# Opening of a two-block transformer kernel: modulation rows loaded ahead of the input

## The chip, the cores and the metric

The kernel runs on one core of a Trainium2 chip. The metric is the device time of one execution in microseconds (us). Three executions of the kernel before took 3241.57, 3241.45 and 3239.81, median 3241.45.

TensorE (PE) multiplies matrices, VectorE (DVE), ScalarE (ACT) and GpSimd (POOL) work elementwise, and SyncE (SP) issues the transfers (DMA). Each engine runs its own instructions in order and waits on semaphores for the others.

## The reference

The model has two blocks over 512 rows of 1024 features. The first holds two layers: an even one (convolution and an RWKV mixer) and an odd one (attention); the second holds a mixer, a product-key expert layer with 16384 experts and a gated embedding. What this case touches is the beginning of the first layer:

```python
cond = jax.nn.silu(c)
mod = cond @ ada_w[l] + ada_b[l]
shift, scale, gate = jnp.split(mod, 3, axis=-1)
h = rms_norm(x, norm_g[l]) * (1.0 + scale[:, None, :]) + shift[:, None, :]
z = h @ even_w_in[j]
```

`cond` is a vector of 1024, `ada_w[0]` is 1024 x 3072, `x` is 512 x 1024, `even_w_in` is 1024 x 7296.

## The kernel before, in words

Features lie on the 128 partitions: `xT` holds the input as eight tiles of 128 x 512. Weights come as units of 128 x 1024 float32, 512 KB each, in the order in which `schedule()` numbers them. That function writes one list of pieces; each engine walks the list and does its own part of each piece, so the list is the order on every engine.

**Modulation rows.** A group `g` of 512 outputs of `cond @ ada_w` takes four units, `ada(0, g)`. TensorE multiplies a unit by two columns of `cond` (line 762, one output row of 512 on a partition, two matmuls a unit, four in the profile). After the fourth unit ACT copies the row (line 1199), TensorE turns it into four columns (line 772, the piece `turned`) and VectorE adds the bias (line 1635). Groups 0 and 1 are the shift, 2 and 3 the scale. So the shift and the scale need 16 units, numbers 0 to 15. `turned_late` puts each `turned` one unit behind its row. The gate's groups 4 and 5 come later.

**Statistics of the input.** For each tile of `xT`, ACT squares (line 1210) and VectorE adds into `msum` (line 1649). `stat` is TensorE's column sum with `ones` (line 782), the mean and root on VectorE and ACT and a diagonal from `ident`; `bcast` spreads it over the partitions (line 791). `norm` is the normalization: for each of eight tiles VectorE scales (line 1697), ACT makes the high part (line 1244), VectorE the low part (line 1709).

**Weights of the dense products.** They are split in a high and a low part: ACT copies the unit as float32r into one of three slots `wsp` (`hi`, line 1178), POOL subtracts (`lo`, line 2439), and TensorE uses three matmuls of 128 x 512 for each of eight blocks (lines 732 to 734). Unit 16 is the mixing product `mu`, units 17, 18 and 19 are `r`, `k` and `v` of head pair 0. ACT's copy of unit n+1 (`hi_to`) stands at the beginning of a piece of unit n, ahead of the copy of a row.

**Places.** The first `NE` = 11 units go to places of their own, in buffers that the RWKV stage uses later (`early`); those behind them go round a ring of `RING` = 3. SP loads units in order (`load_to`, line 2578); a unit from `NE + RING` on waits until the unit three before it has been used. `vec` is the table of all small vectors, `c` among them. `vec`, `ones` and `ident` raise one semaphore, `consts_in`, and their readers wait for all three. Behind `norm` stands `rw_begin`, where VectorE, POOL and SP wait for all engines (`fence`, `all_done`).

Of the kernel before, what the change touches and what calls it, by code (L numbers as in the profile page):

```python
# [20 lines left out]
KT = 8  # L21
CH = 4
# [123 lines left out]
def schedule():  # L146
# [9 lines left out]
    def ada(l, g):  # L156
        return [("ada", l, g, kp, 24 * l + 4 * g + kp) for kp in range(4)]
# [53 lines left out]
    order += [("square", "n0", k) for k in range(KT)]  # L211
    order.append(("stat", "n0"))
    number(ada(0, 0))
    order.append(("bcast", "n0"))
    number(turned_late([x for g in range(1, 4) for x in ada(0, g)], ("turned", 0, 0)))
# [114 lines left out]
    z = [0]  # L330
# [79 lines left out]
def build(nc, t):  # L410
    ORDER, UNITS, FIRST, OF = schedule()
    NU = len(UNITS)
    with ExitStack() as ctx:
# [39 lines left out]
        def chunked(ap):  # L453
            return ap.rearrange("p (c n) -> p c n", c=CH)
# [4 lines left out]
        def kept_set():  # L459
            return {"dd": a(CH), "tt": [chunked(a(512)) for _ in range(3)]}  # L460
# [33 lines left out]
        early = [*(abk[0][:, i * 1024:(i + 1) * 1024] for i in range(4)), *xts, *krs, lup]  # L494
# [94 lines left out]
        consts_in, x_in, rw_in, yc_in, yb_in, ag_in = (sem(f"s_{n}") for n in ("c", "x", "rw", "yc", "yb", "ag"))  # L589
# [134 lines left out]
        def tensor_program(pe):  # L724
# [50 lines left out]
            def stat(tag):  # L775

                out, free = (inv_b if tag == "n0" else all_b).open(("stat", tag), V, "mean", tag)
                w.wait_ge(*free)
                w.wait_ge(consts_in, 48)
                w.wait_ge(vector_done, V("acc", tag, 7))  # L780
                for b in range(4):
                    r = pe.matmul(out[:, b:b + 1], acc_of[tag][:, b * 128:(b + 1) * 128], ones[:, 0:1], start=True, stop=True)
                r.then_inc(tensor_done, T.step("sum", tag))
# [386 lines left out]
        def scalar_program(act):  # L1170
# [15 lines left out]
            def start():  # L1186
                w.wait_ge(consts_in, 48)
                act.activation(cond[:, :], cols("c"), ACT.Silu).then_inc(scalar_done, A.step("cond"))
# [58 lines left out]
            def norm(tag):  # L1247
                shift = {"n0": mod[:, 0, 0:8], "n1": mod[:, 1, 0:8]}.get(tag)
                for k in range(KT):
                    high(tag, k, shift)  # L1250
# [349 lines left out]
        def vector_program(dve):  # L1600
# [22 lines left out]
            def start():  # L1623
                for b in dense.banks:
                    dve.memset(b["ap"], 0.0).then_inc(vector_done, V.step("clear"))
                w.wait_ge(consts_in, 48)
# [941 lines left out]
        def sync_program(sp):  # L2568
# [12 lines left out]
            def start():  # L2581
                sp.dma_start(vec[:, :], t["vec"][:, :]).then_inc(consts_in, 16)
                sp.dma_start(ones[:, :], t["ones"][:, :]).then_inc(consts_in, 16)
                sp.dma_start(ident[:, :], t["ident"][:, :]).then_inc(consts_in, 16)
                sp.dma_start(xT[:, :, :], t["xT"].rearrange("(k p) s -> p k s", p=128)).then_inc(x_in, 16)
# [258 lines left out]
```

## Time and profile before

| | |
|---|---|
| median of 3 runs | 3241.45 us (3239.81 to 3241.57) |
| profiled execution | 3239.83 us, of which its span 3237.9 us |
| TensorE busy | 3065.3 us, 95% |
| VectorE, ScalarE, GpSimd busy | 67%, 38%, 28% |
| mean granted TensorE clock | 0.979 of full speed |
| transferred | 378.81 MB, mean 117 GB/s |

The span begins with the first instruction and ends with the last; times in the profile count from its start. The chain that ended last consists of TensorE for 73% and VectorE for 19%. TensorE's busy share is at least 90% in every fortieth of the span from the fourth on, but for one of 80% and the last of 70%; the first three have 60, 70 and 80%. The granted clock is the share of full speed that the throttle gave TensorE. A timeline row gives start and duration of a merged group of instructions, and in brackets how long the engine sat idle before it and what ended that.

### The profile page before, as it was taken

What the parts mean: (1) busy time and instruction counts of PE and PEld (TensorE: products, weight loads), DVE (VectorE), ACT (ScalarE), POOL (GpSimd) and SP (SyncE); (2) the same over time, 40 slices, a digit from 0 to 9 for tenths busy, and PEclk for the clock granted to TensorE, in tenths of its full rate; (3) what the DMA queues carried; (4) which work ended last, traced back from release to release, by engine and by line L of the source; (5) the groups of instructions that cost most, each with busy time, mean ns of one, the idle gap of its engine ahead of it and who ended that gap; (6) DMA issues with size and microseconds to landing.
All of it is one profiled execution on the core that took longest, in us unless ns stands there. A gap on an engine that the chain in (4) does not pass through costs nothing.

```text
span 3237.9 us, 39785 instructions
## 1 busy us (share of the span) xinstructions
PE 3065.3 (95%) x16086; PEld 2407.6 (74%) x16086; DVE 2184.1 (67%) x3497; ACT 1243.6 (38%) x1815; POOL 892.5 (28%) x550
## 2 busy tenths in 40 slices
PE   6789999999999899999999999999999999999997
PEld 3467776667767566787887788878888888888885
DVE  3688899867789866565889899556665444444454
ACT  3334444435333455323333466532233222233333
POOL 2343343332334110043445433232222111111100
PEclk9999999999999899999999999999999999999999
DMA  5211111235312111232234376775564333333331
GB/s 208 91 69 47 46 46 53 73 105 179 101 65 85 40 39 33 85 117 91 79 130 137 118 235 202 240 247 191 179 201 150 111 119 122 124 123 123 118 117 39
DMA packets 165334, 378.81 MB, mean 117 GB/s; under 512 B 10656, under 2 KB 77216, under 8 KB 165024
## 3 DMA queue, kind: packets, MB, share of 16 engines
q1 hardware_dynamic: 165152, 376.28, 34.6%
q8 instruction: 127, 2.08, 0.3%
q14 instruction: 55, 0.45, 0.0%
HBM read 318.04 MB, written 58.20 MB: 116 GB/s over the span
## 4 chain that ended last, share of the span: by engine, by line
PE 73%; DVE 19%; ACT 4%; POOL 2%; DMA 2%; issue 1%; SPq 0%; DVEq 0%; ACTq 0%; POOLq 0%
PE ps L732 20%; PE ps L734 20%; PE ps L733 20%; DVE rw L1777 3%; DVE oh L2359 2%; PE ps L1121 2%; PE ps L1049 2%; DVE at L2097 2%; DVE ai L2095 1%; PE ps L1029 1%; PE ps L908 1%; DVE at L2085 1%; POOL wsp L2439 1%; POOL pk L2551 1%; PE ps L1039 1%
## 5 line engine op out<-in xcount | busy, mean ns | idle before, releaser
L732 PE MATMUL ps<-hT,wsp 128*128 128x512 f32 x2016 | 825.9, 410 | 35.2 <-POOL wsp L2439 20.1
L2439 POOL TENSOR_TENSOR wsp<-ring,wsp 128x1024 fp32r<-128x1024 f32 x207 | 518.3, 2506 | 1083.9 <-ACT wsp L1178 1060.9
L734 PE MATMUL ps<-hT,wsp 128*128 128x512 f32 x2016 | 793.2, 393 | 0.0
L733 PE MATMUL ps<-hT,wsp 128*128 128x512 f32 x2016 | 792.9, 393 | 0.0
L732 PEld LDWEIGHTS ps<-hT,wsp 128*128 128x128 f32 x2016 | 382.8, 190 | 145.5 <-issue 28.7
L734 PEld LDWEIGHTS ps<-hT,wsp 128*128 128x128 f32 x2016 | 382.6, 190 | 83.6
L733 PEld LDWEIGHTS ps<-hT,wsp 128*128 128x128 f32 x2016 | 383.9, 190 | 77.9 <-issue 6.0
L2558 POOL TENSOR_TENSOR ex<-ex 128x512 fp32r<-128x512 f32 x128 | 176.1, 1390 | 831.4 <-ACT ex L1559 831.4
L1178 ACT ACTIVATE wsp<-ring 128x1024 fp32r<-128x1024 f32 x311 | 322.2, 1051 | 100.8 <-PE ps L734 78.8
L2383 DVE TENSOR_TENSOR xT<-ps,xT 128x512 f32<-128x512 f32 x256 | 174.8, 688 | 261.4 <-PE ps L734 261.4
L732 PE MATMUL ps<-ex 128*128 128x512 f32 x808 | 314.8, 390 | 2.0 <-DVE ex L1611 2.0
L734 PE MATMUL ps<-ex 128*128 128x512 f32 x808 | 315.1, 390 | 0.0
L733 PE MATMUL ps<-ex 128*128 128x512 f32 x808 | 314.6, 389 | 0.0
L1777 DVE SCALAR_TENSOR_TENSOR rw<-rw,vec 128x512 f32<-128x512 f32 x240 | 243.0, 1013 | 5.3
L1178 ACT ACTIVATE ex<-ring 128x1024 fp32r<-128x1024 f32 x121 | 126.2, 1054 | 305.6 <-PE ps L734 197.9
L2373 DVE TENSOR_TENSOR ex<-ex 128x512 f32<-128x512 f32 x128 | 102.8, 824 | 188.1 <-ACT ex L1556 131.1
L1611 DVE TENSOR_TENSOR ex<-ring,ex 128x1024 fp32r<-128x1024 f32 x121 | 164.0, 1355 | 95.6 <-ACT ex L1178 95.6
L732 PEld LDWEIGHTS ps<-ex 128*128 128x128 f32 x808 | 151.8, 188 | 34.8 <-DVE ex L1611 2.8
L733 PEld LDWEIGHTS ps<-ex 128*128 128x128 f32 x808 | 151.8, 188 | 31.9
L734 PEld LDWEIGHTS ps<-ex 128*128 128x128 f32 x808 | 151.8, 188 | 31.6
L1559 ACT ACTIVATE ex<-ex 128x512 fp32r<-128x512 f32 x128 | 80.0, 632 | 240.2 <-DVE ex L2373 240.2
L1611 DVE TENSOR_TENSOR wsp<-ring,wsp 128x1024 fp32r<-128x1024 f32 x104 | 132.0, 1269 | 25.8 <-ACT wsp L1178 25.6
(395 smaller groups left out, 4754.2 us busy)
## 6 DMA issues: line engine op xcount, KB each, us to landing
ring<-in_eu SPq DMA_DIRECT2D x128, 512.0 KB, 3.3
ring<-in_ev SPq DMA_DIRECT2D x128, 512.0 KB, 3.5
gd<-oh SPq DMA_DIRECT2D x8, 4096.0 KB, 15.0
ex<-gd SPq DMA_DIRECT2D x32, 1024.0 KB, 6.6
ring<-in_ein SPq DMA_DIRECT2D x57, 512.0 KB, 3.3
ring<-in_oin SPq DMA_DIRECT2D x39, 512.0 KB, 3.2
ring<-in_ada SPq DMA_DIRECT2D x37, 512.0 KB, 3.2
ex<-zd SPq DMA_DIRECT2D x17, 1024.0 KB, 9.0
```

The source lines that it names most:

```text
L732: pe.matmul(out, W[0], R[0], start=first, stop=False)
L733: pe.matmul(out, W[0], R[1], start=False, stop=False)
L734: return pe.matmul(out, W[1], R[0], start=False, stop=last)
L1049: r = pe.matmul(out, Vs[:, s, :], PTs[h % 2][:, s, :], start=s == 0, stop=s == 3)
L1178: act.activation(split_of(n)[:, 0, :], raw_of(n), ACT.Copy).then_inc(scalar_done, A.step("hi", n))
L1559: act.activation(agb[c % 2][:, 0, j, :], exb[2 + (c * JC + j) % 3], ACT.Copy).then_inc(scalar_done, A.step("agh", c, j))
L1611: dve.tensor_tensor(s[:, 1, :], raw_of(n), s[:, 0, :].bitcast(F32), ALU.subtract).then_inc(vector_done, V.step("lo", n))
L1777: dve.scalar_tensor_tensor(out=y, in0=u[:, k:k + S], scalar=col("conv_w", m * TAPS + k), in1=y, op0=ALU.mult, op1=ALU.add).then_inc(vector ...
L2373: dve.tensor_tensor(exb[2 + i % 3].rearrange("p (b t) -> p b t", t=TG), x.rearrange("p (b t) -> p b t", t=TG), g[:, j, :, :], ALU.mult).th ...
L2383: dve.tensor_tensor(xT[:, dt, :], all_b.at["v", c, dt], xT[:, dt, :], ALU.add).then_inc(vector_done, V.step("v", c, dt))
L2439: pool.tensor_tensor(s[:, 1, :], raw_of(i), s[:, 0, :].bitcast(F32), ALU.subtract).then_inc(pool_done, G.step("lo", i))
L2558: pool.tensor_tensor(agb[c % 2][:, 1, j, :], exb[2 + (c * JC + j) % 3], agb[c % 2][:, 0, j, :].bitcast(F32), ALU.subtract).then_inc(pool_d ...
```

## The change

It has six parts. (1) `vec` gets a semaphore of its own, `vec_in`; the first instructions of ACT (`cond`) and VectorE (`omka`) wait for that, and `stat` waits for the other two constants. (2) SP issues `vec`, units 0 to 4, `xT`, units 5 to 7, `ones`, `ident`, and then the rest. (3) The list has units 0 to 4 and the first `turned` ahead of the squares, units 5 to 12 behind them, then `stat`, units 13 and 14, `bcast`, and unit 15. (4) Three more early places, in the three kept sets of the RWKV stage, whose three 512-column tiles are now one piece of 1536 with the four-column tile behind it; `NE` is 14, so unit 14 is the first in the ring. (5) ACT's next weight copy, of unit 17, stands between the fourth and the fifth tile of `norm`. (6) Line numbers move by two.

```diff
--- before.py
+++ after.py
@@ -208,11 +208,8 @@
     def gates(tiles):
         return [x for m in tiles for x in dense("agate", m, 16 + m)]
 
-    order += [("square", "n0", k) for k in range(KT)]
-    order.append(("stat", "n0"))
-    number(ada(0, 0))
-    order.append(("bcast", "n0"))
-    number(turned_late([x for g in range(1, 4) for x in ada(0, g)], ("turned", 0, 0)))
+    rows = turned_late([x for g in range(4) for x in ada(0, g)])
+    number([*rows[:6], *(("square", "n0", k) for k in range(KT)), *rows[6:15], ("stat", "n0"), *rows[15:18], ("bcast", "n0"), *rows[18:]])
     order.append(("norm", "n0"))
     order.append(("rw_begin",))
     number(dense("mu", 0, 48))
@@ -457,7 +454,8 @@
         a = Stage("rw")
 
         def kept_set():
-            return {"dd": a(CH), "tt": [chunked(a(512)) for _ in range(3)]}
+            turned = a(1536)
+            return {"all": turned, "tt": [chunked(turned[:, i * 512:(i + 1) * 512]) for i in range(3)], "dd": a(CH)}
 
 
         yT, varT, gsT, sgT = (a(512) for _ in range(4))
@@ -491,7 +489,7 @@
                       for i in range(2)) for z in abk]
         XTs = [z.rearrange("p (e c n) -> p e c n", e=2, c=CH) for z in xts[0:2]]
         X = xts[2].rearrange("p (e c n) -> p e c n", e=2, c=CH)
-        early = [*(abk[0][:, i * 1024:(i + 1) * 1024] for i in range(4)), *xts, *krs, lup]
+        early = [*(abk[0][:, i * 1024:(i + 1) * 1024] for i in range(4)), *xts, *krs, lup, *(z["all"][:, 0:1024] for z in sets)]
         NE = len(early)
         Xo = msum.rearrange("p (c e n) -> p c e n", c=CH, e=2)
         Sbd, Su, x1n, SA = (small[:, 2 * i:2 * i + 2, :].rearrange("p a n -> p (a n)") for i in range(4))
@@ -586,7 +584,7 @@
 
         tensor_done, vector_done, scalar_done, pool_done = (sem(f"s_{n}") for n in ("pe", "dve", "act", "pool"))
         T, V, A, G = Marks(tensor_done), Marks(vector_done), Marks(scalar_done), Marks(pool_done)
-        consts_in, x_in, rw_in, yc_in, yb_in, ag_in = (sem(f"s_{n}") for n in ("c", "x", "rw", "yc", "yb", "ag"))
+        vec_in, consts_in, x_in, rw_in, yc_in, yb_in, ag_in = (sem(f"s_{n}") for n in ("vec", "c", "x", "rw", "yc", "yb", "ag"))
         unit_in = [sem(f"s_w{i}") for i in range(RING)]
         early_in = [sem(f"s_e{i}") for i in range(NE)]
         yt_out = [sem(f"s_yt{i}") for i in range(2)]
@@ -776,7 +774,7 @@
 
                 out, free = (inv_b if tag == "n0" else all_b).open(("stat", tag), V, "mean", tag)
                 w.wait_ge(*free)
-                w.wait_ge(consts_in, 48)
+                w.wait_ge(consts_in, 32)
                 w.wait_ge(vector_done, V("acc", tag, 7))
                 for b in range(4):
                     r = pe.matmul(out[:, b:b + 1], acc_of[tag][:, b * 128:(b + 1) * 128], ones[:, 0:1], start=True, stop=True)
@@ -1184,7 +1182,7 @@
                     at["hi"] += 1
 
             def start():
-                w.wait_ge(consts_in, 48)
+                w.wait_ge(vec_in, 16)
                 act.activation(cond[:, :], cols("c"), ACT.Silu).then_inc(scalar_done, A.step("cond"))
 
             def ada(l, g, kp, n):
@@ -1247,6 +1245,8 @@
             def norm(tag):
                 shift = {"n0": mod[:, 0, 0:8], "n1": mod[:, 1, 0:8]}.get(tag)
                 for k in range(KT):
+                    if tag == "n0" and k == 4:
+                        hi_to(at["hi"])
                     high(tag, k, shift)
 
 
@@ -1623,7 +1623,7 @@
             def start():
                 for b in dense.banks:
                     dve.memset(b["ap"], 0.0).then_inc(vector_done, V.step("clear"))
-                w.wait_ge(consts_in, 48)
+                w.wait_ge(vec_in, 16)
                 dve.tensor_scalar(omka[:, :], cols("k_a"), -1.0, 1.0, ALU.mult, ALU.add).then_inc(vector_done, V.step())
 
             def ada(l, g, kp, n):
@@ -2579,10 +2579,12 @@
                     at["load"] += 1
 
             def start():
-                sp.dma_start(vec[:, :], t["vec"][:, :]).then_inc(consts_in, 16)
+                sp.dma_start(vec[:, :], t["vec"][:, :]).then_inc(vec_in, 16)
+                load_to(5)
+                sp.dma_start(xT[:, :, :], t["xT"].rearrange("(k p) s -> p k s", p=128)).then_inc(x_in, 16)
+                load_to(8)
                 sp.dma_start(ones[:, :], t["ones"][:, :]).then_inc(consts_in, 16)
                 sp.dma_start(ident[:, :], t["ident"][:, :]).then_inc(consts_in, 16)
-                sp.dma_start(xT[:, :, :], t["xT"].rearrange("(k p) s -> p k s", p=128)).then_inc(x_in, 16)
                 load_to(NE + RING - 1)
                 sp.dma_start(bones[:, :], t["bones"][:, :]).then_inc(rw_in, 16)
                 sp.dma_start(cen, t["cen"][:, :]).then_inc(rw_in, 16)
```

SP, the queue of transfers, from its beginning; `rw_..` are the early places, and `in_ada` are the row units. Before:

```order
L2582 DMA vec<-in_vec 128x487
L2583 DMA ones<-in_ones 128x128
L2584 DMA ident<-in_ident 128x128
L2585 DMA xT<-in_xT 128x8x512
L2578 DMA rw_43<-in_ada 128x1024 x4
L2578 DMA rw_21<-in_ada 128x1024
L2578 DMA rw_49<-in_ada 128x1024
L2578 DMA rw_22<-in_ada 128x1024
L2578 DMA rw_33<-in_ada 128x1024
L2578 DMA rw_5<-in_ada 128x1024
L2578 DMA rw_34<-in_ada 128x1024
L2578 DMA rw_20<-in_ada 128x1024
```

After:

```order
L2582 DMA vec<-in_vec 128x487
L2578 DMA rw_39<-in_ada 128x1024 x4
L2578 DMA rw_21<-in_ada 128x1024
L2578 DMA rw_43<-in_ada 128x1024
L2584 DMA xT<-in_xT 128x8x512
L2578 DMA rw_22<-in_ada 128x1024
L2578 DMA rw_33<-in_ada 128x1024
L2578 DMA rw_5<-in_ada 128x1024
L2586 DMA ones<-in_ones 128x128
L2587 DMA ident<-in_ident 128x128
L2578 DMA rw_34<-in_ada 128x1024
L2578 DMA rw_20<-in_ada 128x1024
```

Units 0 to 4 have moved ahead of `xT`, and `ones` and `ident` from ahead of `xT` to behind unit 7.

SP again, around the first units of the ring: `in_ein` are the units of the dense products, the first of them 16. Before:

```order
L2578 DMA rw_20<-in_ada 128x1024
L2578 DMA ring<-in_ada 128x1024 x3
L2587 DMA bones<-in_bones 128x128
L2588 DMA rw_29<-in_cen 128x128
L2578 DMA ring<-in_ada 128x1024 [waits s_pe] x2
L2578 DMA ring<-in_ein 128x1024 [waits s_pe] x3
L2578 DMA ring<-in_ein 128x1024 [waits s_pool]
```

After:

```order
L2578 DMA rw_35<-in_ada 128x1024
L2578 DMA rw_40<-in_ada 128x1024
L2578 DMA rw_37<-in_ada 128x1024
L2578 DMA ring<-in_ada 128x1024 x2
L2578 DMA ring<-in_ein 128x1024
L2589 DMA bones<-in_bones 128x128
L2590 DMA rw_29<-in_cen 128x128
```

Before, two row units and the first `in_ein` wait for TensorE; after, only units behind 16 wait.

TensorE, on both sides of the column sums (`msum` and `ones`, 128x1) and of the broadcast (128x512); `s_e0` to `s_e13` are the landings of units 0 to 13. Before, from the beginning of its queue:

```order
L782 MATMUL ps0<-ones,msum 128x1 [waits s_dve,s_c]
L782 MATMUL ps0<-ones,msum 128x1 x3
L762 MATMUL ps6<-rw_43,cond 1x512 [waits s_e0,s_act]
L762 MATMUL ps6<-rw_43,cond 1x512
L762 MATMUL ps6<-rw_43,cond 1x512 [waits s_e1]
L762 MATMUL ps6<-rw_43,cond 1x512
L762 MATMUL ps6<-rw_43,cond 1x512 [waits s_e2]
L762 MATMUL ps6<-rw_43,cond 1x512
L762 MATMUL ps6<-rw_43,cond 1x512 [waits s_e3]
L762 MATMUL ps6<-rw_43,cond 1x512
L791 MATMUL ps1<-msum,ones 128x512 [waits s_dve]
L762 MATMUL ps7<-rw_21,cond 1x512 [waits s_e4]
```

The same engine from unit 11 on. After:

```order
L760 MATMUL ps6<-rw_35,cond 1x512
L760 MATMUL ps7<-rw_40,cond 1x512 [waits s_e12]
L760 MATMUL ps7<-rw_40,cond 1x512
L780 MATMUL ps0<-ones,msum 128x1 [waits s_dve,s_c]
L780 MATMUL ps0<-ones,msum 128x1 x3
L770 MATMUL ps4<-vec,rw_4 128x1 [waits s_act]
L770 MATMUL ps4<-vec,rw_4 128x1 x3
L760 MATMUL ps7<-rw_37,cond 1x512 [waits s_e13]
L760 MATMUL ps7<-rw_37,cond 1x512
L760 MATMUL ps7<-ring,cond 1x512 [waits s_w0]
L760 MATMUL ps7<-ring,cond 1x512
L789 MATMUL ps1<-msum,ones 128x512 [waits s_dve]
```

The column sums have moved from the first place of the queue to behind unit 12 (`s_e12`), and the broadcast from behind unit 3 (`s_e3`) to behind unit 14 (`s_w0`).

ACT, from unit 16's copy (`wsp<-ring`, `s_w2`) through the eight tiles of `norm`. Before:

```order
L1199 ACTIVATE rw_4<-ps6 128x512 [waits s_pe]
L1178 ACTIVATE wsp<-ring 128x1024 [waits s_w2]
L1199 ACTIVATE rw_4<-ps7 128x512 [waits s_pe]
L1244 ACTIVATE hT<-rw_9,mod 128x512 [waits s_pe,s_dve]
L1244 ACTIVATE hT<-rw_10,mod 128x512 [waits s_dve]
L1244 ACTIVATE hT<-rw_24,mod 128x512 [waits s_dve]
L1244 ACTIVATE hT<-rw_4,mod 128x512 [waits s_dve]
L1244 ACTIVATE hT<-rw_9,mod 128x512 [waits s_dve]
L1244 ACTIVATE hT<-rw_10,mod 128x512 [waits s_dve]
L1244 ACTIVATE hT<-rw_24,mod 128x512 [waits s_dve]
L1244 ACTIVATE hT<-rw_4,mod 128x512 [waits s_dve]
L1178 ACTIVATE wsp<-ring 128x1024 [waits s_pool,s_w0,s_act,s_dve]
```

After:

```order
L1215 ACTIVATE cr<-cr 128x4 [waits s_dve]
L1176 ACTIVATE wsp<-ring 128x1024 [waits s_w2]
L1197 ACTIVATE rw_4<-ps7 128x512 [waits s_pe]
L1242 ACTIVATE hT<-rw_9,mod 128x512 [waits s_pe,s_dve]
L1242 ACTIVATE hT<-rw_10,mod 128x512 [waits s_dve]
L1242 ACTIVATE hT<-rw_24,mod 128x512 [waits s_dve]
L1242 ACTIVATE hT<-rw_4,mod 128x512 [waits s_dve]
L1176 ACTIVATE wsp<-ring 128x1024 [waits s_w0]
L1242 ACTIVATE hT<-rw_9,mod 128x512 [waits s_dve]
L1242 ACTIVATE hT<-rw_10,mod 128x512 [waits s_dve]
L1242 ACTIVATE hT<-rw_24,mod 128x512 [waits s_dve]
L1242 ACTIVATE hT<-rw_4,mod 128x512 [waits s_dve]
```

The copy of unit 17 (`s_w0`) stands behind four tiles now, and the copy of unit 18 (`s_w1`) is the first behind the fence.

## Rows read from the trace of the kernel before

**Rows 1.** The page: busy time, share of the span and instructions of TensorE.

```profile
PE 3065.3 (95%) x16086; PEld 2407.6 (74%) x16086; DVE 2184.1 (67%) x3497; ACT 1243.6 (38%) x1815; POOL 892.5 (28%) x550
```

**Rows 2.** Chain of waits, 0 to 120 us: start us, duration us, what.

```profile
2.13 10.48 DMA xT<-in_xT
...
19.49 1.84 PE ps L782 x8
...
21.33 3.44 PE ps L762 x16
...
24.77 1.05 PE ps L791 x2
...
27.76 1.84 PE ps L762 x16
...
39.21 1.06 ACT wsp L1178
...
40.90 1.19 PE ps L772 x8
...
42.75 2.06 DVE rw L1697 x3
...
53.44 1.07 ACT wsp L1178
...
54.67 2.35 POOL wsp L2439
...
57.06 0.50 PE ps L732
...
73.45 0.24 PE ps L734
```

**Rows 3.** Timeline of SP's issues: start us, us, line, transfer, count.

```profile
2.60 0.67 SPq L2578 DMA_DIRECT2D rw<-in_ada  x1
...
13.39 0.44 SPq L2578 DMA_DIRECT2D ring<-in_ada  x1
...
13.87 2.90 SPq L2578 DMA_DIRECT2D ring<-in_ada  x1
...
33.18 0.80 SPq L2578 DMA_DIRECT2D ring<-in_ada  x2
```

**Rows 4.** Transfers issued at 2.60, 13.39, 13.87: size, us to landing.

```profile
rw<-in_ada SPq DMA_DIRECT2D x1, 512.0 KB, 11.3
...
ring<-in_ada SPq DMA_DIRECT2D x1, 512.0 KB, 15.6
...
ring<-in_ada SPq DMA_DIRECT2D x1, 512.0 KB, 16.5
```

**Rows 5.** Timeline of ACT's table load and TensorE's last row units (idle before, releaser).

```profile
16.92 1.28 ACT L1215 ACT_TABLE_LOAD   x1
...
30.27 1.05 PE L772 MATMUL ps<-vec,rw 128*128 128x1 f32 x8 [0.68 <-ACT rw L1199]
...
36.38 1.03 PE L762 MATMUL ps<-ring,cond 128*1 128x512 f32 x4 [0.47 <-DMA ring<-in_ada]
...
37.66 1.03 PE L762 MATMUL ps<-ring,cond 128*1 128x512 f32 x4 [0.25 <-DMA ring<-in_ada]
```

**Rows 6.** Stretches: us, busy (instructions) PE, PEld, DVE, ACT, POOL; PEclk, DMA share, GB/s.

```profile
0.00:5.00 5.00, 0.00 (x0) 0.00 (x0) 0.97 (x2) 1.28 (x1) 0.20 (x4) 1.00 0.51 123
5.00:10.00 5.00, 0.00 (x0) 0.00 (x0) 0.17 (x1) 0.21 (x1) 0.00 (x0) 1.00 1.04 351
20.00:25.00 5.00, 5.00 (x24) 1.93 (x24) 1.03 (x3) 0.33 (x2) 0.00 (x0) 1.00 1.03 419
30.00:35.00 5.00, 3.95 (x34) 2.34 (x36) 0.17 (x2) 0.82 (x2) 0.00 (x0) 1.00 0.15 53
45.00:50.00 5.00, 4.14 (x11) 2.76 (x12) 5.00 (x8) 2.73 (x4) 0.00 (x0) 0.66 0.06 23
```

**Rows 7.** Timeline of ACT in the normalization, one copy of eight.

```profile
46.17 0.72 ACT L1244 ACTIVATE hT<-rw,mod 128x512 fp32r<-128x512 f32 x1 [0.60 <-DVE rw L1697]
```

## The prediction, on record before the changed kernel ran

> **What bounds the kernel now.** I read the page first: TensorE is busy 95% of the span [rows 1], so almost everything after the opening is a line of work behind TensorE, and a few microseconds saved in front of it come out at the end. Then the chain of waits over the first 60 us, where every edit lies [rows 2]. Call the sixteen 512 KB units of the first modulation U0 to U15 and the two weight units behind them U16 (mixing, "mu") and U17 (first r tile). The reader should see four legs. The input lands at 12.6. Squares, their sum and TensorE's column sums end at 21.3, and only then does TensorE begin U0 to U3 (21.33). From there it works through the rows until it reaches units that have not come: U14, U15 and U16 go into the ring of three, and SP issues U14 only at 33.18, when U11 has been used [rows 3]. TensorE starts U14 at 36.38 and U15 at 37.66, both on the DMA [rows 5]. Last, U16 lands at 39.2, ACT copies it (1.06), and only behind that copies the last row; TensorE turns it at 40.90 and the normalization starts at 42.75. It ends at 53.4; then ACT copies U17, POOL subtracts (2.35), and TensorE starts r at 57.06.
>
> So the transfers stand still from about 30 to 33 (0.15 of the DMA engines busy in 30 to 35 [rows 6]), with three units still to come, and TensorE stands idle until 19.5 with units long landed.
>
> **How fast units come.** U0 was issued at 2.60 and landed 11.3 later, 13.9. U12 was issued at 13.39 and took 15.6, landing at 29.0; U13 at 13.87, taking 16.5, at 30.4 [rows 3, 4]. That is (30.4 - 13.9)/13 = 1.27 us a unit, which is 524 KB at the 419 GB/s of the window 20 to 25 [rows 6]. They come in the order of issue: U0 1.3 behind the input.
>
> **The change part by part.**
>
> *Order of the transfers.* What must land before U12 is the same set of bytes before and after: vec, ones, ident, xT, U0 to U12. Only the start differs. In the first 5 us the queue moved 123 GB/s, since three small transfers came first, against 351 in the next 5 [rows 6]. With U0 as the second transfer up to about 3 us of that could run at the higher rate: (351 - 123) x 3 = 0.68 MB at most, from which I allow 0.5 MB, 1.2 us at 419 GB/s. The bounds of this credit are 0 and 1.2; ones and ident still have to pass later, so I take 0.5. U12 lands at 28.5 (27.8 to 29.0). Each further unit adds 1.27 without a wait, because with 14 early places the ring starts at U14 and holds U14, U15, U16: U13 29.8, U14 31.1, U15 32.3, U16 33.6, instead of 36.4, 37.7 and 39.2.
>
> *Input behind U4.* It lands five units later less the credit: 12.6 + 5 x 1.27 - 0.5 = 18.5. The column sums, which wait for the sum of squares, began at 19.5, 6.9 behind the landing [rows 2]; now they could from 25.4. The column sums are placed behind U12 (29.4), so 4 us of slack hide this. The two small copies that ACT now makes behind the squares (0.61 each) wait for U7 and U11, not for the squares, and the ACT table load for the root (1.28 [rows 5]) lies behind U11's copy: U11 at 27.2, its matmuls and the copy until 28.8, the load until 30.1, before the column sums end at 31.2. Nothing is added.
>
> *TensorE's line.* From U12 it is in order and full. U12 0.86 (3.44/4, the slow pace at 21.33), column sums 1.84, turning row 2 1.05, U13 and U14 at the fast pace of 0.46 each (1.84/4), broadcast 1.05, U15 alone 1.03 [rows 2, 5]: 28.5 + 0.86 + 1.84 + 1.05 + 0.92 + 1.05 + 1.03 = 35.25. U16's copy on ACT ends at 33.6 + 1.06 = 34.7, so it no longer holds the last row back. ACT copies the row (0.65, of which TensorE's pause of 0.68 before the turning at 30.27 is the mark [rows 5]), 35.9; the turning starts, and the normalization follows 1.85 behind its start (42.75 - 40.90): 37.8. Gain of this leg: 42.75 - 37.8 = 4.95, say 5.0. What is late next is this serial line and no longer a transfer.
>
> *U17's copy among the normalization.* ACT's copies there take 0.72, with 0.60 of idle time between them [rows 7]; a copy of 1.07 [rows 2] between the fourth and the fifth delays the fifth by 1.07 - 0.60 = 0.47, and VectorE reads the fifth only two steps (2.6 us) on. Behind it on ACT's queue stand four more such copies, each with 0.60 to catch up. U17 waits for U14's use (about 33); U14 itself took 3.2 from its issue to TensorE's start [rows 3, 5], so U17 is there by 37, ahead of about 42. Free. At the end POOL starts at 0.1 after the normalization instead of 54.67 - 53.44 = 1.23 after: a gain of 1.1, carried on since TensorE then works without a hole from 57.06 until 73.7 in the chain. If ACT's copy were late, this term would be 0.
>
> *The rest.* The vector semaphore lets ACT and VectorE start on vec alone, before U0 is there: nothing. Waiting for 32 instead of 48 on ones and ident: they now follow U7 and land near 23, needed at 29.4. The kept set with its 4 columns last moves three tiles by 16 bytes; one set loses what another gains in alignment, and no row tells tiles at such offsets apart; I take 0, with -0.3 to +0.3. The ring's slot numbers stay (11 and 14 have the same remainder by 3), so all later loads wait as before.
>
> Sum: 5.0 + 1.1 = 6.1. Against the profiled execution's 3239.83 (span 3237.9) that is 3233.7; the median of the runs shown, 3241.45, lies 1.6 above it, so 3235.4.
>
> Bounds of the unknown terms. Early end: U12 at 27.8, all of TensorE fast; then U16's copy rules (32.9 + 1.06 = 34.0), normalization at 36.5: 6.2 + 1.1 = 7.3. Late end: no credit (29.0) and every piece slow: 0.86 + 1.84 + 1.19 + 1.72 + 2.1 + 1.03 + 0.61 + 1.99 = 11.3, so 40.3: 2.4 + 1.1 = 3.5. (2.1 is the broadcast doubled, an estimate from its 1.05.)
>
> **Two rules beside the rows.** The profile grants TensorE its full 2.4 GHz in 20 to 25, yet four units take 3.44 there and 1.84 from 27.76 on [rows 2, 6]; in 45 to 50, behind a pause, the granted clock is 0.66. The Trainium skill (TensorE: Matmul & The Clock Gate, Part 1) says that the array is at 1.2 GHz by default and activity releases it, and that the recorded clock events can't be fully trusted. By that rule work that comes in short bursts, as the rows now do, could stay slow to the end of the line, which is rival B; the slow pace at 21.33 agrees.
>
> The Trainium skill (DMA: Bandwidth & Descriptors, Where 436 GB/s comes from) puts a core's limit from HBM at about 358 GB/s. The trace disagrees with 419. By the rule a unit would cost 1.46 instead of 1.27, and U16 would come 0.8 later against U12, still ahead of the last row's copy or level with it.
>
> **The rivals.**
> A. TensorE is fast when U12 comes. For it: at the slow pace it has holes of only 0.4 in the 1.27 us of a unit, and from 27.76 to 38.7 it paused as much and stayed fast [rows 2, 5]. Then the column sums take about 1.0, the line ends at U16's copy (34.7), the copy of the row at 35.3, normalization at 37.2: 5.55 + 1.1 = 6.65, and up to 7.3 with the credit. 3234.8.
> B. TensorE stays slow over the whole line. For it: idle from about 10 to 19 between U4 and U5, and short bursts after. Against: from U12 on it is busy without a hole, and at 21.3 the same sort of work became fast within 5 us. With the slow pieces of the late end, 28.5 + 11.3 = 39.8: 2.95 + 1.1 = 4.0. 3237.4.
> C. The opening gives nothing: the transfers end when they did, slowed by the matmuls that now read units while others land, and only U17's copy pays: 1.1, 3240.3. Against it: in 20 to 25 TensorE was busy throughout and the queue moved 419 GB/s [rows 6].
> D. Slower: the input starves behind and among eleven queued units. If it shared the queue with the nine units issued behind it instead of coming in order, its landing L would drive everything: L + 6.9 (sum of squares), + 1.84 + 1.05 + 0.92 + 1.05 + 1.03 + 0.65 + 1.85 = L + 15.3. That equals 42.75 + 1.1 at L = 28.6; with all units landing first, L is about 33.6, normalization at 48.9, 6.1 - 1.1 = 5.0 slower: 3246.5. Against it: the input landed 1.3 before U0 with eleven units behind it [rows 2, 4].
>
> **How the numbers follow.** The forecast has 0.50, A 0.22, B 0.18, C 0.06, D 0.04. The forecast's own range, with the 1.8 us between the three runs shown, is 3234.0 to 3236.8. For 8 in 10 it reaches through A and B with their spread: 3232.4 to 3238.6. A measurement of this kernel can tell about 0.2%, 6.5 us, from no change; that bound lies at 3235.0, just inside the forecast. Faster: 0.33 of the forecast, three quarters of A and a little of B: 0.40. Slower: 0.03. Same: 0.57.
>
> **What would show it.** U14's matmuls start without a DMA wait other than the pace, by about 33; U16 lands near 33.6; column sums start behind U12 near 29.4; the normalization starts near 37.8, ends 10.7 later; POOL's first subtraction of r starts within 0.2 of its end; r near 51. It would be wrong if the normalization starts outside 36.5 to 40.3, if the pace of landing differs from 1.27, if TensorE's clock falls for long behind 51, or if the time from r's first matmul to the end differs by over 2 us.

## The result, and the profile after

Eight executions of the changed kernel took 3223.62 to 3240.20 us, median 3228.4. Eight of the kernel before took 3232.87 to 3242.44, median 3238.36 (the three shown ahead of the prediction are among them). The ratio is 0.9975, interval 0.9964 to 0.9986, which is 8.1 us less (4.5 to 11.7); the two medians by themselves differ by 10.0. The profiled execution took 3233.98 against 3239.83, with spans of 3232.1 and 3237.9.

The forecast was 3235.4 (3232.4 to 3238.6) and a gain of 6.1. The time lies below the range, and the gain is one that a measurement tells from no change, to which the prediction gave 0.40.

In code line 762 is now 760, 772 is 770, 782 is 780, 791 is 789, 1199 is 1197 and 1178 is 1176; lines 732 to 734 are 730 to 732. The page's span, its line of busy times, and the granted clock in 40 slices. The mean granted clock of this execution was 0.975, where it was 0.979 before, and TensorE's busy time is 13.2 us longer:

```profile
span 3232.1 us, 39783 instructions
...
PE 3078.5 (95%) x16086; PEld 2413.8 (75%) x16086; DVE 2176.2 (67%) x3497; ACT 1243.6 (38%) x1815; POOL 891.8 (28%) x550
...
PEclk9889999999999999999999999999999999999999
```

The chain of waits of the changed kernel (start us, duration us, what), which answers to [rows 2]:

```profile
18.84 13.57 DMA ring<-in_ein
...
32.44 1.06 ACT wsp L1176
...
33.49 0.49 ACT rw L1197
...
34.03 1.07 PE ps L770 x8
...
35.32 0.63 DVE gsc L1639
...
35.97 2.06 DVE rw L1697 x3
...
46.76 2.38 POOL wsp L2439
...
49.18 0.50 PE ps L730
```

The input and TensorE's column sums are gone from the chain. It now consists of SP's issues one after the other from 0.74 to 18.84, the transfer of U16 (issued 18.84, landed 32.4), ACT's copy of U16, its copy of the row behind it, the turning, VectorE, and the normalization, which starts at 35.97 instead of 42.75: 6.8 us earlier. From the normalization's start to r's first matmul it takes 13.2 instead of 14.3, so r starts at 49.18 instead of 57.06: 7.9 us, which the measured 8.1 agrees with.

TensorE's timeline (start, duration, line, matmuls and count, in brackets the idle time and what ended it), to compare with [rows 5] and the slow start at 21.33 in [rows 2]:

```profile
4.78 1.87 PE L760 MATMUL ps<-rw,cond 128*1 128x512 f32 x4 [4.78 <-DMA rw<-in_ada]
...
12.88 1.03 PE L760 MATMUL ps<-rw,cond 128*1 128x512 f32 x4
...
19.39 3.62 PE L760 MATMUL ps<-rw,cond 128*1 128x512 f32 x12 [5.48 <-DMA rw<-in_ada]
...
27.33 1.03 PE L760 MATMUL ps<-rw,cond 128*1 128x512 f32 x4 [0.25 <-DMA rw<-in_ada]
...
28.29 1.05 PE L780 MATMUL ps<-ones,msum 128*128 128x1 f32 x8
...
31.13 1.13 PE L789 MATMUL ps<-msum,ones 128*128 128x512 f32 x2
...
32.19 1.03 PE L760 MATMUL ps<-ring,cond 128*1 128x512 f32 x4
```

U0 lands at 4.7, 3.5 us behind its issue. Six row units are issued ahead of the input, not five: `load_to(5)` loads U0 to U5, and TensorE works on the sixth at 12.88, before the input lands. In the same way `load_to(8)` puts `ones` and `ident` behind U8, not U7. The description of the change and the prediction have both wrong by one unit. U12 is there at 27.33 (forecast 28.5), the column sums take 1.05 and not 1.84, and U15 ends at 33.2 (forecast 35.3).

The stretches that answer to the first and the third of [rows 6] (busy of PE, PEld, DVE, ACT, POOL; granted clock, DMA share, GB/s):

```profile
0.00:5.00 5.00, 0.22 (x2) 0.12 (x4) 1.14 (x3) 1.49 (x2) 0.20 (x4) 1.00 0.65 200
20.00:25.00 5.00, 4.90 (x26) 1.34 (x24) 4.25 (x8) 2.96 (x6) 0.00 (x0) 0.80 1.03 408
```

In the first 5 us the queue moves 200 GB/s instead of 123. TensorE has paused from 13.9 to 19.4 and its granted clock is 0.80 in 20 to 25, but when U12 comes it works at the fast pace.

### The profile page after: what moved, and what is told of

It reads as the page before. It is cut to its first block, busy times and chain, and to the rows that moved or that the text cites. A ratio compares the mean times of both kernels' runs of the same rounds, so it can differ in the third digit from the quotient of the medians.

```text
span 3232.1 us, 39783 instructions
## 1 busy us (share of the span) xinstructions
PE 3078.5 (95%) x16086; PEld 2413.8 (75%) x16086; DVE 2176.2 (67%) x3497; ACT 1243.6 (38%) x1815; POOL 891.8 (28%) x550
## 4 chain that ended last, share of the span: by engine, by line
PE 71%; DVE 19%; ACT 4%; POOL 2%; DMA 2%; issue 1%; SPq 1%; DVEq 0%; ACTq 0%
PE ps L730 20%; PE ps L732 19%; PE ps L731 19%; DVE rw L1777 3%; DVE oh L2359 2%; PE ps L1119 2%; PE ps L1047 2%; DVE at L2097 2%; DVE ai L2095 1%; PE ps L1027 1%; PE ps L906 1%; DVE at L2085 1%; POOL wsp L2439 1%; POOL pk L2551 1%; PE ps L1037 1%
```

## The experiments

All of them are compared by two numbers: the start of r's first matmul in one profile, which an opening moves, and the timed difference to the kernel before on the same chip, with its interval. Single executions of a kernel here differ by up to 19 us (28 to 32 executions of the kernel before beside each group of experiments: 3230.2 to 3249.7), so the timed differences have intervals of 3.2 to 4.9 us to either side. The profiles scatter too. In the five that begin with the same nine units and the input, and in which TensorE waits for U12, U12's matmuls start from 27.2 to 28.1 (with the later start of one of them taken off), and the two profiles of the changed kernel have r at 49.18 and 49.67. One profile tells differences of 1 us and more, not of tenths.

### The changed kernel again

No edit.

> The changed kernel once more. Both theories: r's first matmul at 49.2 us, as in its first profile (57.06 before). They part in the stretch from there to ACT's table load of line 1275, which took 52.3 us before and 55.8 in the first profile of the changed kernel, with TensorE's granted clock at half from 82.9 to 97.4. Theory 1 (the opening's 7.9 us reach the end, and where the clock falls behind it differs from one execution to the next): this profile may show either length, and the timed difference to the kernel before is near -8. Theory 2 (the new opening itself makes the clock fall there and gives 3.5 us back): the stretch is 55 to 56 again and the timed difference is near -4.5.

Measured: ratio 0.9957 (0.9942 to 0.9972), 13.9 us less (9.1 to 18.8). r starts at 49.67. Here TensorE was slow ahead of U12 (granted clock 0.50 in 20 to 25 and 0.66 in 25 to 30), its line ended behind ACT's copy of U16, and the normalization followed TensorE:

```profile
32.62 1.06 ACT L1176 ACTIVATE wsp<-ring 128x1024 fp32r<-128x1024 f32 x1 [1.42 <-DMA ring<-in_ein]
33.26 1.03 PE L760 MATMUL ps<-ring,cond 128*1 128x512 f32 x4
...
36.47 2.06 DVE L1697 SCALAR_TENSOR_TENSOR rw<-xT,gsc,ps 128x512 f32<-128x512 f32 x3
```

That is 3.85 from the start of the copy to the normalization, where the first profile has 3.53.

The stretch from r's start to ACT's table load of line 1275 took 55.0 (55.8 in the first profile of the changed kernel). That looked like theory 2, but the timed difference is far from the 4.5 us that it asks for, and the other kernels settle it. The stretch came out as 52.3 in the kernel before, 51.9, 51.9, 51.9, 53.2 and 53.4 in five others, and 55.1, 55.1, 55.1, 55.1 and 56.6 in five, among these one with the opening time of before (the old list, below: 55.1). So it comes out short or long whatever the opening. In the changed kernel and then in the kernel before, the stretches at the same place of the program:

```profile
80.00:85.00 5.00, 2.12 (x12) 0.18 (x6) 0.00 (x0) 0.00 (x0) 0.00 (x0) 0.85 0.72 253
85.00:90.00 5.00, 4.03 (x9) 1.33 (x6) 1.23 (x2) 4.02 (x5) 2.34 (x1) 0.50 0.49 175
90.00:95.00 5.00, 5.00 (x17) 4.33 (x16) 3.56 (x6) 0.38 (x1) 2.37 (x1) 0.50 0.51 161
95.00:100.00 5.00, 5.00 (x19) 4.00 (x19) 4.79 (x10) 0.00 (x0) 1.83 (x2) 0.79 0.10 40
```

```profile
92.00:97.00 5.00, 3.44 (x6) 0.59 (x6) 0.69 (x1) 3.29 (x4) 2.31 (x1) 0.66 0.65 237
```

After TensorE's pause at this place (it waits for a modulation unit) the granted clock is half, for some 14 us in the changed kernel and 3.4 in the kernel before. These times are estimates from the mean granted clock of the stretch, with the two levels 0.5 and 1. The same working for all thirteen profiles orders them: 3.3 or 3.4 us at half clock in the four whose stretch took 51.9 to 52.3, 6.8 in the six with 53.2 to 55.1, and 10.3 to 13.7 in the three with 55.1, 55.8 and 56.6.

### The whole opening 7 us later

```diff
 def start():                       # VectorE
+    for _ in range(2):
+        dve.memset(abk[0], 0.0).then_inc(vector_done, V.step("late"))
+        own()
 def start():                       # SP
+    w.wait_ge(vector_done, V("late"))
     sp.dma_start(vec[:, :], ...)
```

> The changed kernel with its whole opening pushed back: VectorE first fills a 128x4096 tile twice (3.5 us each), and SP issues nothing before that. No other instruction moves. Theory 1 (a shift of the opening reaches the end whole): r's first matmul near 56.2, 7 us later, and a time 7 us above the changed kernel, about that of the kernel before (difference to it -1). Theory 2 (the shift is partly given back or lost behind the opening): a time 3 to 4 above the changed kernel.

Measured: r starts at 58.32, 9.1 later than in the changed kernel and 1.3 later than before; VectorE's two fills come ahead of everything and took more than I had allowed. Timed 0.9991 (0.998 to 1.0001), 2.9 us below the kernel before (-6.5 to +0.3). The changed kernel gained 13.9 beside it, so a delay of the opening does reach the end; the intervals are too wide to say that all of it does.

### The old list with the new transfers

```diff
-rows = turned_late([x for g in range(4) for x in ada(0, g)])
-number([*rows[:6], *(("square", "n0", k) ...), *rows[6:15], ("stat", "n0"), *rows[15:18], ("bcast", "n0"), *rows[18:]])
+order += [("square", "n0", k) for k in range(KT)]
+order.append(("stat", "n0"))
+number(ada(0, 0))
+order.append(("bcast", "n0"))
+number(turned_late([x for g in range(1, 4) for x in ada(0, g)], ("turned", 0, 0)))
 def stat(tag):                     # ACT
+    w.wait_ge(consts_in, 32)
```

> The changed kernel's transfers, places and semaphores with the old list: squares and column sums ahead of the first row unit on TensorE. With the input landing at 18.1 the column sums begin at 25.0, and the 15 row units behind them go at the pace of before, slow for the first four. Theory 1 (the new place of the row units in the list carries the gain, the transfers alone would lose): normalization from 44.4 instead of 36.0, r from 57.6, a time 8.4 above the changed kernel and 0.5 above the kernel before. Rival (transfers alone carry it, since U16's landing at 32.4 is what bounds): normalization within 1 of 36.0.

Measured: 1.0003 (0.9991 to 1.0015), no gain. r at 57.22. From its chain and TensorE's timeline:

```profile
24.76 1.84 PE ps L783 x8
...
44.01 2.06 DVE rw L1701 x3
...
26.53 3.23 PE L763 MATMUL ps<-rw,cond 128*1 128x512 f32 x16
```

The column sums begin at 24.76 and take 1.84, the first four units take 3.2, and the normalization starts at 44.01 (44.4 expected). The new transfers and places with the old list lose 1.3 us at that point; with the old list, the old transfers and the places alone (below) it starts at 38.30. The list is what makes the new order of transfers pay.

### The two constants first again

```diff
 sp.dma_start(vec[:, :], ...).then_inc(vec_in, 16)
+sp.dma_start(ones[:, :], ...).then_inc(consts_in, 16)
+sp.dma_start(ident[:, :], ...).then_inc(consts_in, 16)
 load_to(5)
 sp.dma_start(xT[:, :, :], ...)
 load_to(8)
-sp.dma_start(ones[:, :], ...).then_inc(consts_in, 16)
-sp.dma_start(ident[:, :], ...).then_inc(consts_in, 16)
```

> The changed kernel with the two constants of 64 KB (ones, ident) issued right behind vec again instead of behind U8. Theory 1 (the small transfers at the beginning cost the first 5 us their rate, and their going away is the missing 1.2 us of credit): U12 lands at 28.5 instead of 27.3, and r starts 1.2 later, 50.4. Rival (they cost what their 128 KB are worth, 0.3 us, or the two issues of 0.47, and the credit has another source): U12 at 27.3 to 27.9 and r at 49.2 to 49.9.

Measured: 0.9976 (0.9965 to 0.9986), r at 51.70, 2.5 later than in the changed kernel. Its stretches 3 to 4 and 20 to 25:

```profile
3.00:4.00 1.00, 0.00 (x0) 0.00 (x0) 0.17 (x1) 0.21 (x1) 0.00 (x0) 1.00 0.36 78
20.00:25.00 5.00, 3.72 (x12) 0.28 (x12) 3.35 (x5) 4.82 (x9) 0.00 (x0) 0.52 1.03 419
```

The same stretch 3 to 4 in the changed kernel:

```profile
3.00:4.00 1.00, 0.00 (x0) 0.00 (x0) 0.17 (x1) 0.21 (x1) 0.00 (x0) 1.00 1.00 385
```

Its U12, U15 and `gsc`:

```profile
28.78 1.03 PE L760 MATMUL ps<-rw,cond 128*1 128x512 f32 x4 [0.25 <-DMA rw<-in_ada]
...
35.28 1.03 PE L760 MATMUL ps<-ring,cond 128*1 128x512 f32 x4
...
38.29 0.17 DVE L1639 SCALAR_TENSOR_TENSOR gsc<-mod,vec 128x8 f32<-128x8 f32 x1
```

U12 comes at 28.78, 1.45 later than in the changed kernel and 0.7 to 1.6 later than in the five profiles above: theory 1, with its size open. Between 3 and 4 the queue moves 78 GB/s, where the changed kernel moves 385. The other profiles bear that out: 108, 115 and 131 in the three others with the constants in front, 356 to 420 in the seven with row units there. Over the first 25 us the mean is 341 GB/s against 350, though, which is 0.2 MB or 0.55 us at the pace; where the rest of the 1.45 comes from is open. The other microsecond of r has another cause: TensorE's granted clock is 0.66 in 30 to 35, where U13, U14 and the broadcast run, so U15 starts at 35.28 and the normalization 1.1 later than U16's landing asks for (ACT's copy at 33.85 + 3.53 = 37.4; it starts at 38.49).

### Without the copy of unit 17 in the normalization

```diff
 for k in range(KT):
-    if tag == "n0" and k == 4:
-        hi_to(at["hi"])
     high(tag, k, shift)
```

> The changed kernel without the copy of unit 17 between the fourth and the fifth tile of the normalization. Theory (the copy is free there and saves ACT's copy behind the end): normalization starts at 36.0 and ends near 46.7 as in the changed kernel, POOL's subtraction starts 1.23 behind its end instead of 0.1, r's first matmul at 50.3 instead of 49.2. Rival (the copy costs VectorE something inside): the normalization is shorter than 10.7 and r is at 49.9 or less.

Measured: 0.9989 (0.9976 to 1.0002). The normalization starts at 36.92 and r at 51.24, which is 14.3 behind it, as before the change; with the copy it is 13.2. So the term of 1.1 holds. The late start of the normalization goes with the clock again (0.66 granted in 30 to 35), from TensorE's timeline:

```profile
31.02 1.91 PE L789 MATMUL ps<-msum,ones 128*128 128x512 f32 x2
...
32.86 1.87 PE L760 MATMUL ps<-ring,cond 128*1 128x512 f32 x4
```

The broadcast and U15 take 1.91 and 1.87, where the changed kernel takes 1.13 and 1.03.

### Eleven early places

```diff
-early = [..., *krs, lup, *(z["all"][:, 0:1024] for z in sets)]
+early = [..., *krs, lup]
```

> The changed kernel with 11 early places instead of 14, so that U14, U15 and U16 wait for the use of U11, U12 and U13. Theory (places matter since the ring's waits stop the transfers): U11 is used at 27.1, U14 is there 3.2 later at 30.4, U15 at 31.7; U13 is used only at 30.6, behind the column sums, so U16 comes at 33.9 instead of 32.4; normalization 3.54 behind that, 37.4, r 50.7. Rival (TensorE's line hides it): normalization within 0.5 of 36.0.

Measured: 0.9997 (0.9985 to 1.0009), r at 52.42, 3.2 later. From its chain:

```profile
31.72 3.95 DMA ring<-in_ein
...
35.69 1.06 ACT wsp L1176
...
39.22 2.06 DVE rw L1697 x3
```

U16 is issued when U13 has been used, at 31.72, and lands at 35.7. I had expected 33.9: U13 used at 30.6 and 3.2 for the transfer. It was used 1.1 later, and the transfer took 3.95. The mechanism is the theory's, its size 1.8 larger.

### The input first

```diff
-load_to(5)
 sp.dma_start(xT[:, :, :], ...)
```

> The changed kernel with the input issued right behind vec, ahead of all row units; list, places and semaphores as in the changed kernel. Theory 1 (the sum of bytes until U16 counts, not which come first; the list does the rest): input at 11.5, U0 at 12.8, U12 at 27.3, U16 at 32.4, normalization at 36.0 to 36.5. Theory 2 (rows ahead of the input are needed, since TensorE is idle for longer and slow when U12 comes, or ACT's first row copy holds the squares up): normalization at 37.5 or later.

Measured: 0.9967 (0.9954 to 0.9979), r at 49.98. TensorE's U0 and U12, and the chain:

```profile
12.63 4.88 PE L760 MATMUL ps<-rw,cond 128*1 128x512 f32 x16 [12.63 <-DMA rw<-in_ada]
...
28.17 1.03 PE L760 MATMUL ps<-rw,cond 128*1 128x512 f32 x4 [0.25 <-DMA rw<-in_ada]
...
33.23 1.06 ACT wsp L1176
...
36.77 2.07 DVE rw L1697 x3
```

U0 comes at 12.63 instead of 4.78, and all that it costs is 0.8 us, the 0.8 by which U12 and U16 come later. That is hardly more than equal openings differ by (U16's copy at 33.13 in the kernel with unit 16 on VectorE, below, and at 33.23 here), so a cost isn't shown. The order of the list counts, with enough units behind the input; which transfer is first counts for less than 1 us.

### Column sums, broadcast and the last row's copy earlier

```diff
-number([*rows[:6], ..., *rows[6:15], ("stat", "n0"), *rows[15:18], ("bcast", "n0"), *rows[18:]])
+number([*rows[:6], ..., *rows[6:13], ("stat", "n0"), *rows[13:15], ("bcast", "n0"), *rows[15:]])
 def ada(l, g, kp, n):              # ACT, for the unit (0, 3, 3)
-    hi_to(n + 1)
     ... act.activation(rowT, ...)
+    hi_to(n + 1)
```

> The changed kernel with the column sums behind U10 and the broadcast behind U12, and ACT's copy of the last row ahead of its copy of U16. Theory (what bounds the changed kernel is U16's landing at 32.4, its copy and the row's copy behind it): U15 lands at 31.2 and is used by 32.3, its row is copied by 32.9, the turning takes 1.05, normalization at 35.0 instead of 36.0, r at 48.2; a time 1 below the changed kernel, which the timing can't tell. Rival (U16's copy, now later, holds the first mu product back): normalization early but r not.

Measured: 0.9976 (0.9963 to 0.9989), r at 49.22: nothing gained. The turning does start 1.4 earlier, but:

```profile
33.62 2.34 POOL L2443 TENSOR_TENSOR wsp<-ring,wsp 128x1024 fp32r<-128x1024 f32 x1 [33.17 <-ACT wsp L1176]
...
33.93 2.04 DVE L1643 SCALAR_TENSOR_TENSOR gsc<-mod,vec 128x8 f32<-128x8 f32 x1
...
36.01 2.06 DVE L1701 SCALAR_TENSOR_TENSOR rw<-xT,gsc,ps 128x512 f32<-128x512 f32 x3
```

The small `gsc` operation of VectorE (128x8) takes 2.04 us and ends with POOL's subtraction of U16. In the kernel before and in the changed kernel:

```profile
40.35 2.34 POOL L2439 TENSOR_TENSOR wsp<-ring,wsp 128x1024 fp32r<-128x1024 f32 x1 [39.91 <-ACT wsp L1178]
...
42.31 0.40 DVE L1639 SCALAR_TENSOR_TENSOR gsc<-mod,vec 128x8 f32<-128x8 f32 x1
```

```profile
33.57 2.34 POOL L2439 TENSOR_TENSOR wsp<-ring,wsp 128x1024 fp32r<-128x1024 f32 x1 [33.13 <-ACT wsp L1176]
...
35.32 0.62 DVE L1639 SCALAR_TENSOR_TENSOR gsc<-mod,vec 128x8 f32<-128x8 f32 x1
```

It takes 0.40 and 0.62 there, and each time the normalization starts within 0.06 us of POOL's end (42.69 and 42.75, 35.91 and 35.97). In the kernel with the constants first, POOL is done before, and it takes 0.17 (row above). The Trainium skill (SBUF — State Buffer, SBUF: two separate sides) says that an operation of VectorE with two inputs in SBUF and a GpSimd operation that reads SBUF exclude each other, and the later one waits to the end. The trace agrees: `gsc` reads `mod` and `vec`, both in SBUF, and the operation just before it, with one input in PSUM, took 0.16 beside the same subtraction.

### Unit 16 subtracted on VectorE

```diff
-on_pool = {n for n, (name, u) in enumerate(UNITS) if by_pool(name, u)}
+on_pool = {n for n, (name, u) in enumerate(UNITS) if by_pool(name, u) and n != 16}
```

> The changed kernel with the subtraction of unit 16 on VectorE instead of POOL (1.27 us instead of 2.34). In the changed kernel POOL subtracts from 33.57 to 35.91, VectorE's gsc of 128x8 begins at 35.32 and takes 0.62, and the normalization starts at 35.97. Theory (a two-input operation of VectorE waits until POOL's subtraction ends): without POOL there gsc takes 0.17, as where POOL is idle, and the normalization starts at 35.5; r's first matmul at 48.75. The time 0.4 below the changed kernel, which the timing can't tell. Rival (gsc's length has another cause): gsc 0.6 and 35.97 again.

Measured: 0.9981 (0.9971 to 0.9991). VectorE:

```profile
34.22 1.23 DVE L1611 TENSOR_TENSOR wsp<-ring,wsp 128x1024 fp32r<-128x1024 f32 x1 [2.71 <-ACT wsp L1176]
...
36.01 0.17 DVE L1639 SCALAR_TENSOR_TENSOR gsc<-mod,vec 128x8 f32<-128x8 f32 x1
...
36.21 2.06 DVE L1697 SCALAR_TENSOR_TENSOR rw<-xT,gsc,ps 128x512 f32<-128x512 f32 x3
```

`gsc` takes 0.17, the normalization follows at once. U16 landed 0.7 later in this execution (ACT's copy at 33.13 instead of 32.44); from that copy to the normalization it takes 3.08 instead of 3.53, the 0.45 expected. r starts at 49.43, and the timing can't tell this kernel from the changed one.

### The places alone, and with the copy

```diff
-early = [..., *krs, lup]
+early = [..., *krs, lup, *(z["all"][:, 0:1024] for z in sets)]   # and the kept sets' new layout
 # the second kernel also:
+    if tag == "n0" and k == 4:
+        hi_to(at["hi"])
```

> The kernel before with the three early places alone (and the new layout of the kept sets that makes room for them). Theory: U14, U15 and U16 follow U13 (30.4) at the pace, 31.7, 33.0 and 34.2, so TensorE has no wait and ends U15 at 35.9; ACT's copy of the row until 36.5, turning, and POOL, which subtracts from 35.4 to 37.7, holds VectorE until then: normalization at 37.8 (42.75 before), r at 52.1. Rival (places bring nothing while the list keeps TensorE back): normalization later than 41.

> The kernel before with the three early places and the copy of unit 17 between the fourth and the fifth tile; transfers, semaphores and list as before. Theory (the parts add): normalization at 37.8, r 1.1 earlier than with the places alone, 51.0; the rest of the changed kernel, its order of transfers and list, is then worth 51.0 - 49.2 = 1.8 us.

Measured: 0.9984 (0.9972 to 0.9997) and 0.9987 (0.9976 to 0.9998). With the places alone the normalization starts at 38.30 and r at 52.61, 4.45 earlier than in the kernel before. From there:

```profile
33.77 1.06 ACT L1179 ACTIVATE wsp<-ring 128x1024 fp32r<-128x1024 f32 x1 [0.70 <-DMA ring<-in_ein]
...
36.84 1.02 PE L773 MATMUL ps<-vec,rw 128*128 128x1 f32 x8 [0.79 <-ACT rw L1200]
...
38.10 0.17 DVE L1640 SCALAR_TENSOR_TENSOR gsc<-mod,vec 128x8 f32<-128x8 f32 x1
...
38.30 2.06 DVE L1698 SCALAR_TENSOR_TENSOR rw<-xT,gsc,ps 128x512 f32<-128x512 f32 x3
```

U16 is there at 33.8 and no longer bounds; TensorE's line behind the late column sums does. In the second kernel everything on TensorE ran 0.7 later, so r is at 52.2 where 51.0 was expected; from the normalization to r it takes 13.2 instead of 14.3, so the copy is worth 1.1 here too. With that the changed kernel divides into 4.45 for the places, 1.1 for the copy and the remaining 2.3 for the order of transfers and list together. This division holds in this order only: with the new list and transfers in place the three places are worth 3.2 (eleven places, above).

### All of them together

The timed difference to the kernel before against the shift of r's start, both in us: changed kernel -8.1 at -7.9 and -13.9 at -7.4; column sums earlier -7.8 at -7.8; unit 16 on VectorE -6.2 at -7.6; input first -10.7 at -7.1; no copy -3.6 at -5.8; constants first -7.8 at -5.4; places and copy -4.2 at -4.9; eleven places -1.0 at -4.6; places -5.2 at -4.45; old list +1.0 at +0.2; 7 us later -2.9 at +1.3. A straight line through the twelve has slope 0.97, and they scatter about it by 2.8, of the size of their intervals. So what the opening gains comes out at the end, within what these timings can tell.

The record shows what the scatter goes with: the mean granted clock, which stands there for every execution of these groups. Over the 89 executions of the kernel before, the time is 2.3 us lower for every 0.001 that the clock is higher (correlation -0.93 within the groups). The two kernels that gained least for their openings, no copy and eleven places, ran at 0.9764 and 0.9763 on average, the kernel before beside them at 0.9784. At that slope this is some 4.7 us, an estimate, and more than the 2.2 and 3.6 by which their times fall short of their openings. Whether such a clock belongs to a kernel or to the moment isn't shown.

## Why the prediction was wrong

The cause was right, the transfers that stood still and TensorE's wait for the input, and so was the sign. The step that failed is the size of two terms of the sum: the credit at the start, taken as 0.5 us and 1.7 in the trace, and TensorE's line, taken as 6.75 and 5.9 in the trace.

- *How fast units come.* Right: (32.44 - 27.33)/4 = 1.28 us a unit from U12 to U16.
- *The credit at the start, 0.5 us.* Too small, and the larger error: U12 came at 27.33, 1.7 before its 29.0, and U16 with it 1.2 before its 33.6 (in the other profiles with this opening U12's credit is 0.9 to 1.8). I kept most of it back for `ones` and `ident`, which still have to pass later. Put back in front they go with a U12 that is 1.45 us later, and behind U8, inside a full queue, next to nothing shows: 365 GB/s over 5 to 15, 371 in the kernel that has them in front. The upper bound of 1.2 came from 3 us at the rate of 5 to 10, 351 GB/s, and was itself too low; the actual rate of 3 to 4 was 385.
- *TensorE's line, 6.75 us from U12 to the end of U15.* It took 5.9. I took U12 and the column sums (1.84) from the slow pace at 21.33, and they ran at the fast one (1.05). That was rival A, at 0.22. The pauses before did lower the clock (0.80 in 20 to 25, 0.52 with the constants first). Of nine profiles with the new list TensorE was slow again at the end of the line in two, about 1.0 us lost (constants first, no copy), and slow ahead of U12 in one, 0.3 lost (the changed kernel again). So rival B's mechanism is there too, in some executions.
- *What is late next.* I named the serial line. In the first profile it is U16's landing, ACT's two copies, and then POOL's subtraction, which the prediction didn't have at all: it lies on the path already before the change (`gsc` 0.40 instead of 0.17). In the three profiles with a slow TensorE it is the serial line.
- *U17's copy, 1.1.* Right, to a tenth, in three pairs.
- *The input behind the rows, and its slack of 4 us.* Right: landed at 18.1 (18.5 forecast, with one unit more ahead of it), the sum of squares was done by 24.8, and the column sums began at 28.3.
- *The rest at nothing.* Nothing in the traces speaks against it. That the vector semaphore brings the first instructions from 5.07 to 3.31 is of use only because U0 is there at 4.7.
- *The sum:* 6.1 forecast, 7.9 in the trace: 1.2 of the difference is the landing, 0.6 the rest of the way from there to the normalization.
- *The signs of being wrong.* The prediction named four, and three came. The normalization started at 35.97, outside 36.5 to 40.3. The clock fell for long behind 51, for some 14 us. And the time from r's first matmul to the end of the span differs by 2.1 us (3180.8 before, 3182.9 after), just over its 2.
- *The absolute time and the range.* I took the spread of a kernel from three runs, 1.8 us. Eight runs of the same kernel spread over 9.6, and the median of the kernel before itself moved from 3241.45 to 3238.36. With that median the forecast's gain would have given 3232.3. Of the 7.0 us by which the absolute time missed, 3.1 are this, 1.8 are the two terms, and the remaining 2.1 (the medians differ by 10.0, the openings by 7.9) lie within the interval.
- *Rival C and D.* C would have left the opening where it was, and it moved by 6.8. The input landed at 18.1 and U6 at 19.4, in the order of issue, where D had it last.

What stays open: why the changed kernel came out at -8.1 on one chip and at -13.9 on another, at openings 0.5 apart. The intervals overlap (4.5 to 11.7 and 9.1 to 18.8), and the plain medians differ by 10.0 and 11.9, so there may be nothing to explain. The stretch behind r and the granted clock show one source of such scatter; that it explains the rest was not shown. The 2.3 us that list and transfers share are not divided either: no run has the new list with the transfers of before. The nearest is the input first with the new list, which has r only 0.8 later than the changed kernel.

## What to carry to other kernels

Look for a queue of transfers that stands still while units are still to come, and for a list in which the engines take what has landed. Here the places alone brought U16 5.4 us forward (39.2 to 33.8) and gave 4.45 us of 7.9 even with the old list; the new order of transfers with the old list lost. When a small operation on VectorE takes several times its usual length, look at what POOL does at that moment before moving anything ahead of it. And take the spread of a kernel from more than three runs before a range rests on it, with the mean granted clock of each beside its time.

## What the runs showed of the hardware

- With two transfers of 64 KB in rows of 512 B among the first three, the queue moved 78 to 131 GB/s in the stretch 3 to 4 (four profiles), with 512 KB units there 356 to 420 (seven). U12 came at 28.8 in the kernel that differs in nothing else, and at 27.2 to 28.1 without them.
- A VectorE operation of 128x8 with two inputs took 0.17 us alone and 2.04 beside a POOL subtraction of 2.34, ending with it.
- TensorE's granted clock fell to half behind a pause at one place of the program in all thirteen profiles, and stayed there for 3.4 us in some and 13.6 in another, with the same instructions (estimates from mean granted clocks); the stretch behind r's start came out at 52 to 57 us, longer where the half clock lasted longer.
- Executions of one kernel on one core differed by up to 19 us, and their times went with the mean granted clock: 2.3 us for 0.001.
- The queue moved 417 GB/s in 15 to 20 of the kernel before, with TensorE idle until 19.5, and 419 in 20 to 25, with TensorE busy throughout.
